# Modulation tiles summed by TensorE next to VectorE, and the opening loads in another order, in a two-layer decoder trunk

## The reference, cut to what matters

```python
cond = jax.nn.silu(c)
for layer in range(DEPTH):
    mod = cond @ ada_w[layer] + ada_b[layer]
    shift, scale, gate = jnp.split(mod, 3, axis=-1)
    h = rms_norm(x, norm_w[layer]) * (1.0 + scale[:, None, :]) + shift[:, None, :]
    y = moba_branch(h, ...) if layer % N_MIXERS == 0 else mlstm_branch(h, ...)
    x = x + gate[:, None, :] * y
```

## Time and profile before

| | us |
|---|---|
| median of 3 runs (lowest to highest) | 1510.14 (1509.96 to 1510.31) |
| the profiled execution | 1509.85 |
| its span in the trace | 1508.1 |
| TensorE busy | 1446.5 (96%) |
| VectorE busy | 1105.2 (73%) |
| ScalarE busy | 744.5 (49%) |

### The profile page before, as it was taken

One profiled execution on the slowest core, in us unless ns is written; L12 is line 12 of the kernel. 1 busy time (PEld: TensorE's weight loads), 2 busy tenths in 40 slices (PEclk: granted clock), 3 DMA queues, 4 the chain that ended last, 5 costly groups with the idle time before them and its releaser, 6 DMA issues.

```text
span 1508.1 us, 19057 instructions
## 1 busy us (share of the span) xinstructions
PE 1446.5 (96%) x6679; PEld 1198.7 (79%) x6679; DVE 1105.2 (73%) x1234; ACT 744.5 (49%) x1002; POOL 41.7 (3%) x78
## 2 busy tenths in 40 slices
PE   2889999999999989899999999999999999999998
PEld 2767888888888867688888888888888888888886
DVE  5999899989898875878766566566566666656657
ACT  3544646454446455544544544544554454554452
POOL 1000110101000000000000000000000000000000
PEclk9999999999999999999999999999999999999999
DMA  9999889998989735798766566556566566566553
GB/s 338 386 393 391 269 282 339 324 327 287 336 294 353 263 114 183 254 310 300 251 184 187 174 191 185 173 189 188 174 194 181 173 191 193 167 189 190 178 182 112
DMA packets 199230, 361.47 MB, mean 240 GB/s; under 512 B 14224, under 2 KB 48360, under 8 KB 199164
## 3 DMA queue, kind: packets, MB, share of 16 engines
q1 hardware_dynamic: 198112, 359.60, 72.3%
q10 hardware_dynamic: 1056, 1.06, 0.2%
HBM read 358.51 MB, written 2.11 MB: 239 GB/s over the span
## 4 chain that ended last, share of the span: by engine, by line
PE 76%; issue 10%; DVE 7%; ACT 3%; DMA 2%; SPq 1%; POOL 0%; ACTq 0%; DVEq 0%; POOLq 0%
PE proj L1336 23%; PE proj L1338 22%; PE proj L1337 22%; DVE ada_acc L853 4%; PE mix L1336 1%; PE mix L1338 1%; PE mix L1337 1%; DVE w_lo L834 1%; DMA raw<-in_att_w_in 1%; DMA ada_more<-in_ada_w 1%; ACT w_hi L563 1%; PE mix L1455 1%; PE mix L1522 1%; PE mix L1570 1%; ACT work L646 1%
## 5 line engine op out<-in xcount | busy, mean ns | idle before, releaser
L834 DVE TENSOR_TENSOR w_lo<-raw,w_hi 128x1024 fp32r<-128x1024 f32 x480 | 585.5, 1222 | 355.5 <-ACT w_hi L563 354.8
L563 ACT ACTIVATE w_hi<-raw 128x1024 fp32r<-128x1024 f32 x480 | 507.4, 1061 | 682.5 <-PE proj L1338 570.5
L1336 PE MATMUL proj<-w_hi,h_hi 128*128 128x512 f32 x1472 | 583.7, 397 | 7.1 <-DVE h_lo L906 3.9
L1338 PE MATMUL proj<-w_hi,h_lo 128*128 128x512 f32 x1472 | 575.2, 391 | 0.0
L1337 PE MATMUL proj<-w_lo,h_hi 128*128 128x512 f32 x1472 | 574.6, 390 | 0.0
L1336 PEld LDWEIGHTS proj<-w_hi,h_hi 128*128 128x128 f32 x1472 | 277.7, 189 | 66.9 <-issue 9.1
L1338 PEld LDWEIGHTS proj<-w_hi,h_lo 128*128 128x128 f32 x1472 | 277.1, 188 | 58.6
L1337 PEld LDWEIGHTS proj<-w_lo,h_hi 128*128 128x128 f32 x1472 | 277.7, 189 | 57.6 <-issue 1.4
L853 DVE SCALAR_TENSOR_TENSOR ada_acc<-ada_raw,cond,ada_acc 128x1024 f32<-128x1024 f32 x148 | 188.9, 1276 | 2.8 <-DMA ada_raw<-in_ada_w 1.8
L1336 PE MATMUL proj<-w_hi,y_hi 128*128 128x512 f32 x320 | 126.0, 394 | 1.3 <-DVE stream L1004 1.3
L1338 PE MATMUL proj<-w_hi,y_lo 128*128 128x512 f32 x320 | 124.6, 389 | 0.0
(11 more groups left out here) (202 smaller groups left out, 936.5 us busy)
## 6 DMA issues: line engine op xcount, KB each, us to landing
raw<-in_mlstm_w_in SPq DMA_DIRECT2D x192, 512.0 KB, 3.7
ada_raw<-in_ada_w SPq DMA_DIRECT2D x160, 512.0 KB, 6.0
raw<-in_att_w_in SPq DMA_DIRECT2D x128, 512.0 KB, 7.1
raw<-in_mlstm_w_in SPq DMA_DIRECT2D x128, 256.0 KB, 3.0
raw<-in_mlstm_w_out SPq DMA_DIRECT2D x64, 512.0 KB, 4.3
raw<-in_att_w_out SPq DMA_DIRECT2D x32, 512.0 KB, 6.1
ada_more<-in_ada_w SPq DMA_DIRECT2D x16, 512.0 KB, 10.9
work<-in_ada_w SPq DMA_DIRECT2D x16, 512.0 KB, 10.6
```

The lines of the kernel that those rows point to most:

```text
L563: act.activation(w_hi[:, c % LEAD, :], raw[:, c % LEAD, :], ACT.Copy).then_inc(hi_ready, 1)
L834: dve.tensor_tensor(w_lo[:, c % LEAD, :], raw[:, c % LEAD, :], w_hi[:, c % LEAD, :].bitcast(F32), ALU.subtract).then_inc(lo_ready, 1)
L1336: pe.matmul(out_, a_hi, b_hi, start=start, stop=False, **kw)
L1338: return pe.matmul(out_, a_lo, b_hi, start=False, stop=stop, **kw)
```

## The change

1. **Tiles on TensorE.** `BY_PE` names tiles that DVE no longer takes: k-tiles 3, 5, 8, 14 and 15 of block 0, and 13, 14, 15 of blocks 1 and 2. For each, `mod_part` runs eight matmuls with the raw tile itself as the weights and its column of `cond` as the one moving column, into eight columns of its own in bank `mix[3]`. Such a tile's slot is freed by TensorE (`ada_pe`, or `ada_summed` for k-tile 15). `mod_sum` is now `mod_taken` (the eight matmuls of before) followed by the block's parts; DVE adds the columns up with two `tensor_reduce` in `mod_evac`. Block 3 and the blocks of layer 1 stay as they were.
2. **x second.** SP issues tile 0, the bias, the four chunks of `x`, then tiles 1 to 15. Each chunk has a semaphore of its own, and ACT squares a chunk when it is in.
3. **Small loads on ACT's queue.** `c`, the constants, norm weights, norm rows and conv rows are issued by ACT.
4. **Conv rows short.** The conv rows come as 128 rows of 512 bytes into `work` and are turned by one transpose in place of 32. `raw` is free from the start.
5. The places of `norm_sum` and `norm_scale` on DVE, and the banks of the turned `x`, are moved to suit.

```diff
-        conv_rows = raw[:].rearrange("p l n -> p (l n)")[0:TAPS, 0:2 * QK1]
+        conv_rows = work[:, 9344:9472]
...
+        BY_PE = {0: (3, 5, 8, 14, 15), 1: (13, 14, 15), 2: (13, 14, 15)}
+        def by_pe(n):
+            return n % KT in BY_PE.get(n // KT, ())
+        def taken(n):
+            return sum(not by_pe(i) for i in range(n))
...
+        def slot_free(sp, n):
+            if by_pe(n) and n % KT == KT - 1:
+                sp.wait_ge(ada_summed, n // KT + 1)
+            elif by_pe(n):
+                sp.wait_ge(ada_pe, turned(n + 1))
+            else:
+                sp.wait_ge(ada_tile, taken(n + 1))
...
         def sp_program(sp):
-            sp.dma_start(rows_c, c[0].rearrange("(t p) -> t p", p=P)).then_inc(c_in, 16)
-            sp.dma_start(const[:], consts[:, 0:C_COS]).then_inc(consts_in, 16)
-            sp.dma_start(rows_n, norm_w.rearrange("l (t p) -> (l t) p", p=P)).then_inc(c_in, 16)
+            load_ada(sp, 0)
             sp.wait_ge(bias_zeroed, 1)
-            for n in range(KT):
+            sp.dma_start(ada_bias[0:1], ada_rows[0:1, 0:2, 0:NC]).then_inc(ada_bias_in, 16)
+            for q in range(CHUNKS):
+                sp.dma_start(stream[:, :, q * NC:(q + 1) * NC], x_v[:, :, q * NC:(q + 1) * NC]).then_inc(x_in[q], 16)
+            for n in range(1, KT):
                 load_ada(sp, n)
...
-            sp.wait_ge(conv_turned, 1)
...
         def mod_evac(dve, bank, k, layer, b):
...
+            if k in BY_PE:
+                sums = mix[bank][:, 0:8 * (1 + len(BY_PE[k]))].rearrange("p (i j) -> p j i", j=8)
+                scale = scale_sum[:]
+                dve.tensor_reduce(scale, sums[:, 4:8], AX.X, ALU.add).then_inc(scale_added, 1)
+                dve.tensor_reduce(shift_flat[:, at], sums[:, 0:4], AX.X, ALU.add)
...
             for n in range(KT):
-                take_ada(dve, n)
+                if not by_pe(n):
+                    take_ada(dve, n)
...
+        def mod_part(pe, k, t):
+            n = k * KT + t
+            at = 8 * (1 + BY_PE[k].index(t))
+            pe.wait_ge(ada_in[slot_of(n)], slot_fills(n) * 16)
+            for j in range(8):
+                op = pe.matmul(mix[3][:, at + j:at + j + 1],
+                               ada_slot[slot_of(n)][:, j // 4, j % 4 * P:(j % 4 + 1) * P],
+                               cond[:, t:t + 1], start=True, stop=True)
...
+        def mod_sum(pe, k):
+            mod_taken(pe, k)
+            for t in BY_PE.get(k, ()):
+                mod_part(pe, k, t)
...
             pe.wait_ge(cond_ready, 1)
+            mod_part(pe, 0, 3)
+            mod_part(pe, 0, 5)
             pe.wait_ge(xn_act, CHUNKS)
             pe.wait_ge(xn_dve, CHUNKS)
-            for q in range(UNIT):
+            for q in range(4):
                 turn_x(pe, 0, q)
-            pe.wait_ge(xnT_act, 4)
-            mod_sum(pe, 3, 0, 0)
+            mod_part(pe, 0, 8)
+            for q in range(4, UNIT):
+                turn_x(pe, 0, q)
+            mod_taken(pe, 0)
+            mod_part(pe, 0, 14)
+            mod_part(pe, 0, 15)
```

More of the change, by code:

```diff
@@ L332, in build @@
         v1_hi_ready, pT1_hi_ready = (sem(n) for n in ("v1_hi_ready", "pT1_hi_ready"))
-        c_in, conv_turned, norm_turned = (sem(n) for n in ("c_in", "conv_turned", "norm_turned"))
+        c_in, conv_turned, norm_turned, ada_pe, scale_added = (sem(n) for n in (
+            "c_in", "conv_turned", "norm_turned", "ada_pe", "scale_added"))
         raw_in = [ctx.enter_context(nc.semaphore(f"raw_in{i}")) for i in range(LEAD)]
@@ L358, in fills, with turned @@
             return it * (BODY // LEAD + sum(n % LEAD == c % LEAD for n in body)) + sum(1 + two_loads(n) for n in same)
+        BY_PE = {0: (3, 5, 8, 14, 15), 1: (13, 14, 15), 2: (13, 14, 15)}
[3 more added lines that the diff above has]
+            return sum(not by_pe(i) for i in range(n))
+        def turned(n):
+            return sum(by_pe(i) and i % KT < KT - 1 for i in range(n))
         MOD, GATE = 0, 1
@@ L483, in load_ada @@
                 [slice(2, 3), slice(b * 2 * NC, (b + 1) * 2 * NC)]
-            if n % KT == 0:
-                wait(sp, ada_tile, n - KT + 1)
+            if n and n % KT == 0:
+                wait(sp, ada_tile, taken(n - KT + 1))
                 bias = ada_bias[0:1] if kind == MOD else ada_bias[0:1].rearrange("p s n -> p (s n)")
                 sp.dma_start(bias, ada_rows[layer:layer + 1, cols[0], cols[1]]).then_inc(ada_bias_in, 16)
-            wait(sp, ada_tile, n + 1 - (ADA_START if n < ADA_LATE + ADA_SLOTS else ADA_SLOTS))
+            before = n - (ADA_START if n < ADA_LATE + ADA_SLOTS else ADA_SLOTS)
+            if before >= 0:
+                slot_free(sp, before)
             dst = ada_slot[slot_of(n)]
@@ L1231, in dve_program @@
                 {i + 1: [lambda k=k: mod_evac(dve, 3, k, 1, k - 4)] for i, k in SUM_MOD1.items()},
-                {i: [lambda n=n: take_ada(dve, n) for n in ns] for i, ns in TAKES0.items()},
+                {i: [lambda n=n: take_ada(dve, n) for n in ns if not by_pe(n)] for i, ns in TAKES0.items()},
                 {-4: [lambda: h_rest(dve, 0, 1)]},
@@ L1430, in turn_rows @@
             pe.transpose(proj[0][1][:, 128:160], rows_v, ident[0:32, 0:32])
[L1431 to L1434, removed]
+            pe.transpose(proj[0][1][:, 0:P], conv_rows, ident).then_inc(conv_turned, 1)
         def turn_x(pe, layer, q):
@@ L1439, in turn_x @@
             pe.wait_ge(xn_dve, CHUNKS * layer + q // 2 + 1)
+            if layer == 0 and q == 7:
+                pe.wait_ge(xnT_act, 1)
             if layer and q >= 4:
```

59 lines of the change are left out of this document (35 added, 24 removed).

## The result

The changed kernel takes **1522.31 us** (median of 4 runs, 1521.26 to 1524.02), the kernel before, in the same session, 1510.22 (4 runs, 1509.96 to 1510.74). The ratio is 1.0079, 95% interval 1.0067 to 1.0091. Slower was forecast, but only 1515.0 with a range up to 1519: the direction held, the size did not. The profiled execution took 1521.3 us, its span is 1519.5, 11.4 above before.

What follows compares the result with a forecast made beforehand. DMA and VectorE were full from 44 to 152 us, TensorE bound from 165. H of 2.9 less two sums of 9.9 put granule 22 5.0 us later, kept to the end: 1515.0 us, likely 1512 to 1518, range 1508 to 1519.

Steps and rivals of the forecast that it cites:

- the two grown sums with the granules behind them: Behind granules 10 and 21: each sum with its parts costs 9.9 us, the granule behind about 1.6 us more.
- the head start H: Loads: the full DMA rate begins 2.9 us earlier (1.0 to 3.9), and only this survives at granule 8.
- the start of granule 0: End of the opening: granule 0 starts near 39.6 instead of 44.08, a gain of 4.5 us that isn't passed on.
- Rival A: Sums of blocks 1 and 2: the clock stays up, the sums cost 6.8 us, total 1508.1 us; chance 0.24.
- The fall at 41.14: Kernel before, opening: clock fell after a sum and 0.5 us standstill; taken to show one-column matmuls don't help the clock.
- Rival C: SP's loads wait for slots held by parts and DMA runs empty: about 1518 to 1520 us; chance 0.09.
- Rival B: SP's later loads are issue-bound, H could reach 5.2 (granule 8 at 63.3), clock falling: 1512.8 us; chance 0.12.
- The term for the conv rows: Loads at 10 to 12 us: the four long rows hold DMA at 175 GB/s; shortening them gives 1.1 us of H.
- The term of 1.5 for the first load: First 6 us: SP's first 512 KB load goes out 2.2 us earlier, of which 1.5 counts towards H.
- `mod_taken` and parts 14 and 15 end at about 37: Block 0's sum with its last two parts in the opening ends at about 37, against 40.7 for the sum before.
- it then falls 3.7 us in (the mean): Both grown sums: clock falls 3.7 us in (bounds 2.2 and 5.2), the remaining 3.1 us of groups take twice as long.
- about 1.6 us more: The granule behind a grown sum (11, 22) runs at the low clock, costing about 1.6 us above 2.72.

Runs made afterwards that it cites:

- e7_conv: The kernel before with part 4 of the change alone (short conv rows, one transpose, raw free from the start): 1510.25 us, ratio 0.9997.
- e9_two: e2_noparts with the three parts of blocks 1 and 2 put back, none in block 0: 1519.87 us, ratio 1.0060 to the kernel before.
- e5_warm: The changed kernel with four extra wide matmuls ahead of each part in blocks 1 and 2: 1529.79 us, ratio 1.0118 to the kernel before.
- e2_noparts: The changed kernel with no parts on TensorE, VectorE taking all tiles, loads in the new order: 1509.81 us, ratio 0.9993 to the kernel before.
- e3_one: The changed kernel with one part (k-tile 15) instead of three in blocks 1 and 2: 1514.02 us, ratio 1.0013 to the kernel before.
- e10_single: e2_noparts with one part (k-tile 15) in each of blocks 1 and 2: 1510.49 us, ratio 0.9997 to the kernel before.

## Why the prediction was right or wrong

The forecast had the direction and the mechanism, and was too small by 6.4 us in the trace: 5.0 forecast, 11.4 measured. The term that was mis-sized most is the two grown sums with the granules behind them, 2.9 us; then come the head start H, 1.45, the start of granule 0, 0.6 at granule 8, and 1.5 that no term had.

**Right in kind.** The profile forecast what bounded the kernel: with the waits gone TensorE's own time decides, and the clock falls inside the grown sums. Rival A (the clock stays up, 1508.1) is refuted at both places. In the changed kernel TensorE is busy 1.00 in every microsecond around both falls. The fall at 41.14 had pointed that way. The Trainium skill (TensorE: Matmul & The Clock Gate, HAM oscillation) puts such falls down to idle gaps. This trace does not agree: with the gaps closed, the clock fell all the same. Rival C (held slots starve DMA) is refuted as a cause of the loss, since no granule waits: TensorE is busy 108.00 of 108. But the loads did run short: 353 GB/s in place of 390 from 44 to 152 us, and none at all from 136 to 137. Rival B (more of the early start reaches granule 8) failed the other way, less did.

**The head start H was taken as 2.9 and the weights gave 1.45.** ScalarE rounds granule 10 at 64.99 (66.44 before). The term for the conv rows came out near its size: 175 became 407 GB/s, (407 - 175) x 2 / 390 = 1.2 us against 1.1, and e7_conv, with all of part 4, shows 1.26. The term of 1.5 for the first load was worth next to nothing: the first 6 us move 167 GB/s in place of 136, which is 0.5 us, but 6 to 10 us move 328 in place of 373, which takes 0.5 back. The step that failed was "Of the 2.2 us I take 1.5", for SP's first load that goes out 2.2 us earlier: an issue that is earlier isn't bytes that move earlier.

**Granule 0 at 43.00, not 39.6.** The step "`mod_taken` and parts 14 and 15 end at about 37" counted them at full clock, 5.1 us from about 31.9. They ran from 32.56 to 40.56, 8.0 us, since the clock fell in them too (PEclk is 0.61 from 35 to 36 us and 0.50 from 36 to 48). The prediction used the fall at 41.14 for blocks 1 and 2 and forgot it for block 0. This is also why granule 8 came at 67.64: ScalarE's copy, for which it waited before, is done at 66.96 (65.96 + 1.00), and TensorE itself arrives 0.7 later, 24.6 us behind granule 0 and not 23.7, since it runs at the low clock for 5.9 us there (until 48.9) and not 3.9. With H this is 2.0 us of the miss.

**The sums: 10.3 and 11.1 in place of 9.9.** The form of the term was right. Behind granule 10 the clock fell 3.8 us in (a mean of 0.80 from 79 to 80), near the 3.7 of the forecast, which was luck given how far the falls scatter; but a full-clock group took 1.8 us, not 1.70. Behind granule 21 it fell 2.65 us in (0.78 from 120 to 121). e9_two has 2.2 (0.68 from 77 to 78 puts it at 77.36, the sum starts at 75.18), e5_warm 3.8: the place of the fall varies from run to run, inside the bounds of 2.2 and 5.2 that the prediction set. Granules 11 and 22 ran longer at half rate than before (granule 11 took 4.57 us, forecast 4.3; granule 22 5.25, until 134.25, while the one of before was back at full clock at 123). That makes +0.4 and +0.3 at the first, +1.2 and +1.0 at the second: 2.9 us. The step that failed here is "it then falls 3.7 us in (the mean)", one figure for both places, and "about 1.6 us more" for the granule behind.

**The rest, 1.5 us,** is mostly the slow GpSimd multiply. e2_noparts has it too (4.83 us, offset +1.4); the other twelve traces, e9_two with its six parts among them (0.51), have 0.22 to 0.76. So it isn't the six parts that bring it; that it comes by chance is argued, not shown. Between the trace and the median another 0.9 us of the miss (1522.31 against 1515.0, 7.3) lies in the other runs. Two of the four have a higher mean clock (0.987 against 0.984) and took 2 to 3 us more, which would fit an opening at half rate as in e3_one; no trace of them shows it.

**The range** was too narrow above: it took the errors of H and of both falls as "less or plus", where all three could be late at once; with H = 1.0 and both falls after 2.2 us the sum itself had +10, which the stated range then cut to about +9.

## What to carry to other kernels

Work given to TensorE because it seems to wait costs its full time as soon as the wait is used up: here the wait of 2 us paid for one part, the second and third came out whole, at about twice their full-clock price. Cost small matmuls at the rate that the granted clock will have by then, and every place of them alike, and charge the granule behind as well. And an earlier start of loads or of the first granule is worth what the next wait downstream leaves of it: in e2_noparts nothing, since a wait for weights at 213 us took back what the opening had won.

## What the runs showed of the hardware

- One-column float32 matmuls keep TensorE busy by the profile (1.00, weight loads 1.00), and yet the granted clock fell from 2.4 to 1.2 GHz during them in both grown sums of the changed kernel and of e9_two, 2.2 to 3.8 us behind the first. The eight of block 3's sum, 1.70 us right between wide matmuls, left it at 1.00. In e10_single behind granule 21 it fell when wide matmuls were already running again (a mean of 0.96 from 119 to 120, 0.50 from 120 on; they began at 118.56).
- PEclk reads 1.00 in the opening (27 to 29 us of e3_one) while a group of one-column matmuls takes 3.41 us, the half-rate price. Until the first change of the clock in a trace the durations tell the level, not the column.
- With one-column matmuls ahead of and between the turns the same opening runs at either rate: granule 0 at 43.18 or 46.74. Ten runs of such versions scatter over 7 to 11 us; with the turns in one piece it was 3.2 to 4.5.
- Four rows of 16 KB on 4 partitions held the DMA engines at 175 GB/s for 2 us with a busy share of 0.99; as 128 rows of 512 bytes they left 307 there (407 where ScalarE issued them early, in the changed kernel).
- The same 128x16 multiply on GpSimd takes 0.22 to 0.76 us in twelve traces and 4.74 and 4.83 in two.
